# Summing the squares of the RMS norms: from adds on VectorE to accumulating matmuls on TensorE

## The chip, the cores and the metric

The kernel runs on one core of a Trainium2 chip. The metric is device time in microseconds of one execution. "Before" is the kernel as it stands, "after" the one with the change.

## What is computed

A two-layer backbone over 512 latent tokens of width 2048, with 256 context tokens. What matters here is its beginning:

```
shift, scale, gate = split(silu(c) @ w_mod + b_mod, 3)
h  = rmsnorm(x,   g) * (1 + scale)   + shift      # 512 tokens
hc = rmsnorm(ctx, g) * (1 + scale_c) + shift_c    # 256 tokens
rmsnorm(x, g) = x * rsqrt(mean(x*x over the 2048 channels) + 1e-6) * g
```

`h` and `hc` then go through the input projection, windowed attention, a Fourier mixer, the output projection, a pooling layer and a last norm. All of it is float32.

## The kernel before

Channels lie on the 128 partitions and tokens on the free axis, so `x` is 16 tiles (`KT`) of 128 x 512 in `main`, and `ctx` 16 tiles of 128 x 256 in `ctx_t`, which is a part of `kvmem`. The sum over the channels of a token is therefore a sum over 16 tiles and over the partitions; the latter is done by a matmul with `ones` (128 x 128).

The kernel begins with the modulation stage. The first 4096 columns of `l0_w_mod` are streamed as 64 units of 512 KB through four slots of `raw`; a column group `cg` (512 columns, 8 in all) has eight units `s`, each with two channel tiles. For each unit TensorE does two matmuls of 32 condition columns (`cond_cols`, two of them in use) against 512 weight columns. They write 32 of the 128 partitions of bank `cg % 2`, so four tiles of channels land in four partition groups. The unit's last matmul increments `mod_used`, and on that SP (line 276) reloads the slot. When a group is done, ScalarE copies the bank to `mod_rows` (L381), and TensorE turns these rows into columns (`turn_rows`, four small matmuls) behind unit `s == 1` of the next group.

In groups 1 to 4 ScalarE also takes the squares of the 32 tiles, eight in each group (`mod_square`, L322): group 1 and 2 those of `x`, 512 columns wide, group 3 and 4 those of the context, 256 wide. The first square of each kind goes straight into `rstd_x` or `rstd_c` (both in `kvmem`), the others into the two buffers of `tmp`, and VectorE adds them up there (L701). `sq_summed` counts these adds and frees the buffers; `summed_before` gives how many adds stand before a tile. TensorE then sums each of the two over the partitions, with one matmul with `ones` behind unit 3 of group 4 and one behind unit 3 of group 6 (`sum_tokens`), into banks 5 and 6. VectorE waits for both (`tokens_summed`), computes 1 / (mean + eps) (`variance`, L623 and L624), and when all groups are done ScalarE takes the roots (L327). Then come the first two weight splits (L316, L576), the shift and scale vectors, and tile by tile the norm (L627), the split of `h` into two parts (L334, L636) and the first projection.

All engines run their own program in the order written; there is no planner. Every matmul is issued from line 925.

Of the kernel before, what the change touches and what calls it, by code (L numbers as in the profile page):

```python
# [26 lines left out]
SEQ = 512  # L27
CTX = 256
KT = D // P
GROUP = 4  # L30
COLS = GROUP * P
HALVES = KT // 2
# [42 lines left out]
ALU = mybir.AluOpType  # L75
ACT = mybir.ActivationFunctionType
# [48 lines left out]
def build(nc, weights, modb, xT, ctxT, vectors, wf, ident_in, identb_in, masks_in, rope_in, dft_tok_in,  # L125
          dft_ch_in, edges_in, outT):
    with ExitStack() as whole:
        def sb(name, shape, dt, scope=whole):
            return scope.enter_context(nc.sbuf_tensor(name, shape, dt))

        def sem(name):
            return whole.enter_context(nc.semaphore(name))
# [10 lines left out]
        tmp = sb("tmp", [P, 2, WIDE], F32)  # L143
# [3 lines left out]
        ones = ones_r[:].bitcast(F32)  # L147
# [43 lines left out]
        def kv_part(at, shape):  # L191
            n = int(np.prod(shape))
            view = kvmem[:, at:at + n]
            return view if len(shape) == 1 else view.rearrange("p (a b) -> p a b", a=shape[0])
# [13 lines left out]
        rstd_x = kv_part(k_kc, [SEQ])  # L208
        rstd_c = kv_part(k_kc + SEQ, [CTX])
# [5 lines left out]
        ps = whole.enter_context(nc.psum_tensor("ps", [P, 8, 512], F32))  # L215
# [18 lines left out]
        ones_ready, own = sem("ones_ready"), sem("own")  # L234
# [3 lines left out]
        rows_ready, rows_turned = sem("rows_ready"), sem("rows_turned")  # L238
        acc_step, acc_reduced, red_free = sem("acc_step"), sem("acc_reduced"), sem("red_free")
        squared, sq_summed, sq_added = sem("squared"), sem("sq_summed"), sem("sq_added")  # L240
        tokens_summed = sem("tokens_summed")
        ssum_done, var_ready, rstd_ready = sem("ssum_done"), sem("var_ready"), sem("rstd_ready")
        hi_ready, lo_ready, weights_used = sem("hi_ready"), sem("lo_ready"), sem("weights_used")
        tile_ready, split_hi, split_done = sem("tile_ready"), sem("split_hi"), sem("split_done")
# [11 lines left out]
        p_hi_ready, p_ready, p_used = sem("p_hi_ready"), sem("p_ready"), sem("p_used")  # L256
        grp_free = sem("grp_free")
        out_ready = sem("out_ready")

        def summed_before(index):  # L260

            return max(index - 1, 0) if index <= KT else index - 2

        block = whole.enter_context(nc.Block())

# [40 lines left out]
        def _(act):  # L306
# [9 lines left out]
                nc.scalar.copy(w_hi[:, j % 2], raw[:, slot]).then_inc(hi_ready, 1)  # L316

            def square(index, x, n):
                first = {0: rstd_x, KT: rstd_c}.get(index)
                if index >= 2 and summed_before(index - 1):  # L320
                    act.wait_ge(sq_summed, summed_before(index - 1))
                nc.scalar.activation(tmp[:, index % 2, 0:n] if first is None else first, x,  # L322
                                     ACT.Square).then_inc(squared, 1)

            def root(k, dst):
                act.wait_ge(var_ready, k)
# [35 lines left out]
            def mod_square(cg, s):  # L362
                if cg not in range(1, 5):
                    return
                index = HALVES * (cg - 1) + s
                if index == 0:
                    act.wait_ge(x_landed, 64)
                if index == KT:
                    act.wait_ge(ctx_landed, 16)
                if index < KT:  # L370
                    square(index, main[:, index], SEQ)
                else:
                    square(index, ctx_t[:, index - KT], CTX)
# [162 lines left out]
            for g in range(GROUP):  # L536
# [5 lines left out]
                for m in range(GROUP):  # L542
                    t = GROUP * g + m
# [26 lines left out]
        def _(dve):  # L570
# [46 lines left out]
            def variance(k, sums, dst, n):  # L617

                if k > 2:
                    dve.wait_ge(ssum_done, k - 2)  # L620
                if k > 1:
                    dve.wait_ge(var_ready, k - 1)
                chain.link(nc.vector.tensor_scalar(scratch[:, 0:n], sums, 1.0 / D, EPS, ALU.mult, ALU.add))  # L623
                nc.vector.reciprocal(dst, scratch[:, 0:n]).then_inc(var_ready, 1)  # L624
# [67 lines left out]
            chain.link(nc.vector.tensor_tensor(sink_lo[:, :, 0], sinks, sink_hi[:, :, 0].bitcast(F32), ALU.subtract))  # L692


            for index in range(2 * KT):
                if index % KT:
                    dst, n = (rstd_x, SEQ) if index < KT else (rstd_c, CTX)
                    dve.wait_ge(squared, index + 1)
                    if summed_before(index):
                        dve.wait_ge(sq_summed, summed_before(index))  # L700
                    nc.vector.tensor_tensor(dst, dst, tmp[:, index % 2, 0:n], ALU.add).then_inc(sq_summed, 1)  # L701
            dve.wait_ge(tokens_summed, 2)
            variance(1, ps[:, 5], rstd_x, SEQ)
            variance(2, ps[:, 6, 0:CTX], rstd_c, CTX)
            lo(G_K, 0)
# [217 lines left out]
        def _(pe):  # L923
            def mm(out, lhsT, rhs, start, stop):
                return nc.tensor.matmul(out, lhsT, rhs, start=start, stop=stop, skip_group_check=True)  # L925
# [56 lines left out]
                mm(ps[:, 5], ones, ssum, True, True).then_inc(ssum_done, 1)  # L982


            def sum_tokens(index, bank, squares, n):
                pe.wait_ge(sq_summed, summed_before(index))
                mm(ps[:, bank, 0:n], ones, squares, True, True).then_inc(tokens_summed, 1)

            def turn_rows(cg):
                pe.wait_ge(rows_ready, cg + 1)  # L990
                for m in range(GROUP):
                    at = (cg * GROUP + m) * 2
                    ins = mm(ps[:, MOD_BANK, at:at + 2], mod_rows[:, m * P:(m + 1) * P],
                             vec[:, V_ID:V_END], m == 0, True)
                ins.then_inc(rows_turned, 1)

            pe.wait_ge(cond_ready, 1)
            for cg in range(MODS):
                for s in range(HALVES):
                    unit_index = cg * HALVES + s  # L1000
                    pe.wait_ge(raw_landed[unit_index % RAW_SLOTS], (unit_index // RAW_SLOTS + 1) * 16)
                    for r in range(2):
                        kt = 2 * s + r
                        rows = slice(32 * (kt % 4), 32 * (kt % 4) + 32)
                        ins = mm(ps[rows, cg % 2], cond_cols[:, kt], raw[:, unit_index % RAW_SLOTS, r],
                                 kt < 4, kt >= KT - 4)
                    ins.then_inc(mod_used, 1)
                    if s == 1 and cg:
                        turn_rows(cg - 1)
                    if s == 3 and cg == 4:  # L1010
                        sum_tokens(KT, 5, rstd_x, SEQ)
                    if s == 3 and cg == 6:
                        sum_tokens(2 * KT, 6, rstd_c, CTX)
            turn_rows(MODS - 1)


# [142 lines left out]
            for g in range(GROUP):  # L1159
                for kt in range(GROUP):  # L1160
                    s = 2 * g + kt // 2
# [111 lines left out]
```

## Time and profile before

| | |
|---|---|
| Time, median of 3 runs | 1673.22 us (1669.27 to 1677.97) |
| Profiled execution | 1669.27 us, span 1667.6 us |
| Mean granted TensorE clock | 0.960 |
| Busy: TensorE, VectorE, ScalarE, GpSimd | 1507.8, 862.8, 514.8, 67.9 us |
| First unit of the modulation stage starts | 22.75 us |
| Copy of its last group | 125.43 us |

The span is the time between the first and the last instruction of the profiled execution; the time has 1.7 us more around it. Busy times of TensorE count pipelined matmuls, whose ends are modelled. Times of rows are from the span's start.

### The profile page before, as it was taken

What the parts mean: (1) busy time and instruction counts of PE and PEld (TensorE: products, weight loads), DVE (VectorE), ACT (ScalarE), POOL (GpSimd) and SP (SyncE); (2) the same over time, 40 slices, a digit from 0 to 9 for tenths busy, and PEclk for the clock granted to TensorE, in tenths of its full rate; (3) what the DMA queues carried; (4) which work ended last, traced back from release to release, by engine and by line L of the source; (5) the groups of instructions that cost most, each with busy time, mean ns of one, the idle gap of its engine ahead of it and who ended that gap; (6) DMA issues with size and microseconds to landing.
All of it is one profiled execution on the core that took longest, in us unless ns stands there. A gap on an engine that the chain in (4) does not pass through costs nothing.

```text
span 1667.6 us, 19661 instructions
## 1 busy us (share of the span) xinstructions
PE 1507.8 (90%) x6928; PEld 1196.8 (72%) x6928; DVE 862.8 (52%) x1249; ACT 514.8 (31%) x741; POOL 67.9 (4%) x132
## 2 busy tenths in 40 slices
PE   3774999999999999999989997699999999989994
PEld 0114888877775888888878885588877888878883
DVE  1218353455654686777675566633448433353335
ACT  1305141234422343433332222322235222242221
POOL 0000000100010000000001000000000000000000
PEclk9997999999999999999999998799999999999997
DMA  9992434644462233333365555122324332222322
GB/s 343 322 321 89 139 119 162 221 152 162 164 199 82 90 114 100 113 102 112 102 229 187 188 178 174 38 89 100 101 75 151 115 101 88 100 76 101 100 76 101
DMA packets 69062, 232.45 MB, mean 139 GB/s; under 512 B 7328, under 2 KB 10400, under 8 KB 68896
## 3 DMA queue, kind: packets, MB, share of 16 engines
q1 hardware_dynamic: 42624, 151.01, 26.5%
q0 software_dynamic: 18432, 67.12, 12.0%
q10 hardware_dynamic: 7968, 13.82, 2.4%
q8 instruction: 23, 0.38, 0.1%
q14 instruction: 15, 0.12, 0.0%
HBM read 227.73 MB, written 4.19 MB: 139 GB/s over the span
## 4 chain that ended last, share of the span: by engine, by line
PE 74%; DVE 13%; DMA 5%; issue 4%; ACT 3%; ACTq 1%; DVEq 0%; SPq 0%; POOLq 0%
PE ps L925 72%; DMA raw<-in_weights 4%; DVE w_lo L576 2%; ACT tmp L405 1%; PE ps L1112 1%; DVE h_lo L636 1%; DVE scratch L586 1%; DMA modchunk<-in_modb 1%; DVE stat L786 1%; DVE tmp L672 1%; DVE tmp L627 1%; DVE tmp L864 1%; DVE main L627 1%; DVE main L918 1%; DVE pt_lo L804 1%
## 5 line engine op out<-in xcount | busy, mean ns | idle before, releaser
L925 PE MATMUL ps<-h_hi,w_hi 128*128 128x512 f32 x1600 | 639.8, 400 | 64.4 <-DVE w_lo L576 32.4
L925 PE MATMUL ps<-h_lo,w_hi 128*128 128x512 f32 x1600 | 631.2, 394 | 0.0
L925 PE MATMUL ps<-h_hi,w_lo 128*128 128x512 f32 x1600 | 631.1, 394 | 0.0
L576 DVE TENSOR_TENSOR w_lo<-raw,w_hi 128x1024 fp32r<-128x1024 f32 x216 | 264.0, 1223 | 552.3 <-ACT w_hi L316 552.0
L316 ACT CAST w_hi<-raw 128x1024 fp32r<-128x1024 f32 x216 | 226.6, 1052 | 749.9 <-PE ps L925 748.2
L925 PEld LDWEIGHTS ps<-h_hi,w_hi 128*128 128x128 f32 x1600 | 305.8, 191 | 130.8 <-issue 34.9
L925 PEld LDWEIGHTS ps<-h_hi,w_lo 128*128 128x128 f32 x1600 | 305.4, 191 | 65.9
L925 PEld LDWEIGHTS ps<-h_lo,w_hi 128*128 128x128 f32 x1600 | 306.2, 191 | 60.1
L586 DVE SCALAR_TENSOR_TENSOR scratch<-modchunk,cond,scratch 128x512 f32<-128x512 f32 x240 | 179.9, 749 | 22.6 <-DMA modchunk<-in_modb 17.1
L291 POOL DMA_DIRECT2D modchunk<-in_modb x128 | 67.7, 529 | 1225.2 <-DVE scratch L586 1096.4
L925 PE MATMUL ps<-raw,kvmem 128*32 128x512 f32 x256 | 68.1, 702 | 48.8 <-DMA raw<-in_weights 25.8
L925 PEld LDWEIGHTS ps<-raw,kvmem 128*32 128x32 f32 x256 | 9.6, 117 | 98.6 <-DMA raw<-in_weights 74.1
L475 ACT CAST pt_hi<-ps 128x512 fp32r<-128x512 f32 (+1 forms) x48 | 30.7, 640 | 121.6 <-PE ps L1112 121.6
L786 DVE TENSOR_REDUCE stat<-ps 128x1 f32<-128x513 f32 (+1 forms) x48 | 36.3, 756 | 35.4 <-PE ps L925 35.1
L925 PE MATMUL ps<-k_hi,q_hi 128*128 128x256 f32 (+1 forms) x96 | 34.4, 359 | 10.1 <-ACT kvmem L479 5.8
L804 DVE TENSOR_TENSOR pt_lo<-ps,pt_hi 128x512 fp32r<-128x512 f32 (+1 forms) x48 | 36.2, 753 | 8.2 <-ACT pt_hi L475 7.7
L701 DVE TENSOR_TENSOR kvmem<-kvmem,tmp 128x512 f32<-128x512 f32 (+1 forms) x30 | 16.8, 559 | 38.6 <-ACT tmp L322 35.9
L925 PEld LDWEIGHTS ps<-k_hi,q_hi 128*128 128x128 f32 x96 | 18.7, 194 | 17.4 <-ACT kvmem L479 9.3
L405 ACT ACTIVATE tmp<-main 32x512 f32 x48 | 30.2, 630 | 0.7
L925 PE MATMUL ps<-p_hi,w_hi 128*128 128x512 f32 x64 | 26.1, 409 | 3.6 <-issue 3.6
L381 ACT COPY kvmem<-ps 128x512 f32<-128x512 f32 x8 | 4.7, 586 | 79.2 <-PE ps L925 79.2
L444 ACT ACTIVATE tmp<-ps 128x512 f32<-128x512 f32 x32 | 19.2, 599 | 31.6 <-PE ps L925 23.5
(148 smaller groups left out, 1370.5 us busy)
## 6 DMA issues: line engine op xcount, KB each, us to landing
raw<-in_weights SPq DMA_DIRECT2D x280, 512.0 KB, 3.3
modchunk<-in_modb POOLq DMA_DIRECT2D x128, 512.0 KB, 3.6
main<-in_xT ACTq DMA_DIRECT2D x8, 1024.0 KB, 9.1
out<-main SPq DMA_DIRECT2D x16, 256.0 KB, 2.3
kvmem<-in_ctxT ACTq DMA_DIRECT2D x1, 2048.0 KB, 17.5
dft_tok<-in_dft_tok ACTq DMA_DIRECT2D x1, 2048.0 KB, 9.1
kvmem<-in_rope ACTq DMA_DIRECT2D x1, 512.0 KB, 16.1
wf_sb<-in_wf ACTq DMA_DIRECT2D x1, 256.0 KB, 4.1
```

Source lines behind the costliest of these rows:

```text
L291: pool.dma_start(modchunk[:, slot].rearrange("p a n -> p (a n)"), src).then_inc(chunk_landed[slot], 16)
L316: nc.scalar.copy(w_hi[:, j % 2], raw[:, slot]).then_inc(hi_ready, 1)
L405: ins = nc.scalar.activation(tmp[q:q + 32, m % 2, 0:SEQ], view(m)[p:p + 32], ACT.Identity)
L444: nc.scalar.activation(tmp[:, m % 2, 0:SEQ], ps[:, m], ACT.Tanh, scale=0.5).then_inc(tanh_done, 1)
L475: nc.scalar.copy(*turned_tiles(k - 1, pt_hi)).then_inc(pt_hi_ready, 1)
L576: nc.vector.tensor_tensor(w_lo[:, j % 2], raw[:, j % RAW_SLOTS], w_hi[:, j % 2].bitcast(F32), ALU.subtract).then_inc(lo_ready, 1)
L586: ins = nc.vector.scalar_tensor_tensor(out=modacc[:], in0=modchunk[:, s % 2, r], scalar=cond[:, kt, 0:1], in1=modacc[:], op0=ALU.mult, op1 ...
L627: nc.vector.scalar_tensor_tensor(out=dst, in0=x, scalar=g, in1=r, op0=ALU.mult, op1=ALU.mult).then_inc(tile_ready, 1)
L701: nc.vector.tensor_tensor(dst, dst, tmp[:, index % 2, 0:n], ALU.add).then_inc(sq_summed, 1)
L786: chain.link(nc.vector.tensor_reduce(stat[:, 0, par:par + 1], ps_flat[:, S_END - width:S_END], AX.X, ALU.max))
L804: nc.vector.tensor_tensor(lo_part, turned_part, hi_part.bitcast(F32), ALU.subtract).then_inc(pt_ready, 1)
L925: return nc.tensor.matmul(out, lhsT, rhs, start=start, stop=stop, skip_group_check=True)
```

## The change

VectorE no longer adds squares, and each square, now always in `tmp`, is summed over the partitions by a matmul with `ones` of its own. The 16 matmuls of a kind accumulate in bank 5 or 6. On TensorE such a matmul stands right behind each unit of groups 1 to 4 and waits for its square; it increments `sq_summed`, on which ScalarE waits before it overwrites a buffer of `tmp`. VectorE waits for `sq_summed` to reach 32. The two sums at groups 4 and 6, the semaphore `tokens_summed` and `summed_before` are gone, and TensorE waits for `ones_ready` once.

```
 # ScalarE
 def square(index, x, n):
-    first = {0: rstd_x, KT: rstd_c}.get(index)
-    if index >= 2 and summed_before(index - 1):
-        act.wait_ge(sq_summed, summed_before(index - 1))
-    nc.scalar.activation(tmp[:, index % 2, 0:n] if first is None else first, x,
-                         ACT.Square).then_inc(squared, 1)
+    if index >= 2:
+        act.wait_ge(sq_summed, index - 1)
+    nc.scalar.activation(tmp[:, index % 2, 0:n], x, ACT.Square).then_inc(squared, 1)
...
 # VectorE
-for index in range(2 * KT):
-    if index % KT:
-        dst, n = (rstd_x, SEQ) if index < KT else (rstd_c, CTX)
-        dve.wait_ge(squared, index + 1)
-        if summed_before(index):
-            dve.wait_ge(sq_summed, summed_before(index))
-        nc.vector.tensor_tensor(dst, dst, tmp[:, index % 2, 0:n], ALU.add).then_inc(sq_summed, 1)
-dve.wait_ge(tokens_summed, 2)
+dve.wait_ge(sq_summed, 2 * KT)
...
 # TensorE
-def sum_tokens(index, bank, squares, n):
-    pe.wait_ge(sq_summed, summed_before(index))
-    mm(ps[:, bank, 0:n], ones, squares, True, True).then_inc(tokens_summed, 1)
+def mod_square(cg, s):
+    if cg not in range(1, 5):
+        return
+    index = HALVES * (cg - 1) + s
+    t, bank, n = (index, 5, SEQ) if index < KT else (index - KT, 6, CTX)
+    pe.wait_ge(squared, index + 1)
+    mm(ps[:, bank, 0:n], ones, tmp[:, index % 2, 0:n], t == 0, t == KT - 1).then_inc(sq_summed, 1)
+
+pe.wait_ge(ones_ready, 1)
...
         ins.then_inc(mod_used, 1)
+        mod_square(cg, s)
         if s == 1 and cg:
             turn_rows(cg - 1)
-        if s == 3 and cg == 4:
-            sum_tokens(KT, 5, rstd_x, SEQ)
-        if s == 3 and cg == 6:
-            sum_tokens(2 * KT, 6, rstd_c, CTX)
```

## Rows read from the trace of the kernel before

**Rows 1.** The page: busy times; TensorE and DMA in tenths of 40 slices.

```profile
PE 1507.8 (90%) x6928; PEld 1196.8 (72%) x6928; DVE 862.8 (52%) x1249; ACT 514.8 (31%) x741; POOL 67.9 (4%) x132
...
PE   3774999999999999999989997699999999989994
...
DMA  9992434644462233333365555122324332222322
```

**Rows 2.** The chain of waits in order of time: start us, us, what.

```profile
36.81 5.08 PE ps L925 x20
42.92 5.55 DMA raw<-in_weights
...
124.33 1.08 PE ps L925 x4
125.43 0.59 ACT kvmem L381
```

**Rows 3.** Stretches of groups 1 to 5: length, busy times, PEclk, DMA share, GB/s.

```profile
34.20:48.51 14.31, 9.83 (x41) 2.59 (x41) 4.85 (x7) 5.46 (x11) 0.00 (x0) 0.88 0.90 318
48.51:61.80 13.29, 10.60 (x41) 2.27 (x41) 5.54 (x8) 4.95 (x9) 0.00 (x0) 0.74 0.90 309
61.80:74.78 12.98, 9.32 (x40) 2.11 (x41) 3.29 (x8) 4.63 (x12) 0.00 (x0) 1.00 0.95 336
74.78:86.86 12.08, 9.83 (x42) 2.42 (x42) 3.09 (x8) 2.93 (x7) 0.00 (x0) 1.00 0.96 341
86.86:99.42 12.56, 9.33 (x40) 2.12 (x40) 0.00 (x0) 0.48 (x2) 0.00 (x0) 1.00 0.93 320
```

**Rows 4.** Timeline: start us, us, instruction, [idle before <-releaser].

```profile
64.02 0.97 PEld L925 LDWEIGHTS ps<-vec,kvmem 128*128 128x128 f32 x8 [0.84 <-issue]
...
78.84 0.14 PEld L925 LDWEIGHTS ps<-raw,kvmem 128*32 128x32 f32 x4 [0.69 <-DMA raw<-in_weights]
79.82 0.30 PEld L925 LDWEIGHTS ps<-kvmem,ones_r 128*128 128x128 f32 x2 [0.84 <-issue]
...
80.88 0.14 PEld L925 LDWEIGHTS ps<-raw,kvmem 128*32 128x32 f32 x4 [0.76 <-DMA raw<-in_weights]
...
93.53 1.05 PE L925 MATMUL ps<-raw,kvmem 128*32 128x512 f32 x4 [0.67 <-DMA raw<-in_weights]
...
105.27 0.30 PEld L925 LDWEIGHTS ps<-kvmem,ones_r 128*128 128x128 f32 x2 [0.84 <-issue]
...
105.90 0.14 PEld L925 LDWEIGHTS ps<-raw,kvmem 128*32 128x32 f32 x4 [0.33 <-issue]
```

**Rows 5.** One load's issue; landing times, 28 to 125 us; waits in groups 1 to 4.

```profile
82.12 0.33 SPq L270 DMA_DIRECT2D raw<-in_weights  x1
...
DMA to landing us min/median/max: 3.2/5.0/6.3
...
PEld ps L925 <- DMA raw<-in_weights: 39.6, 28, 2.8
```

**Rows 6.** ScalarE at a group's border; the adds on VectorE; VectorE's wait.

```profile
60.53 1.05 PE L925 MATMUL ps<-raw,kvmem 128*32 128x512 f32 x4 [0.26 <-DMA raw<-in_weights]
61.63 0.59 ACT L381 COPY kvmem<-ps 128x512 f32<-128x512 f32 x1 [7.27 <-PE ps L925]
...
62.11 0.42 ACT L322 ACTIVATE kvmem<-kvmem 128x256 f32<-128x256 f32 x1
...
L701 DVE TENSOR_TENSOR kvmem<-kvmem,tmp x30: 424/559/694, 35.5 to 78.2; 128x512 f32<-128x512 f32 x15, 128x256 f32<-128x256 f32 x15
...
106.00 0.69 DVE L623 TENSOR_SCALAR scratch<-ps 128x512 f32<-128x512 f32 x1 [27.38 <-PE ps L925]
```

**Rows 7.** Matmuls with `ones` of the later norms: ns min/median/max, first and last start.

```profile
L925 PE MATMUL ps<-ubuf,ones_r x4: 592/879/1222, 1036.1 to 1648.7; 128*128 128x512 f32 x4
```

**Rows 8.** Timeline of the weight loads around 30 us.

```profile
30.08 0.19 PEld L925 LDWEIGHTS ps<-raw,kvmem 128*32 128x32 f32 x4 [1.09 <-DMA raw<-in_weights]
...
31.36 0.19 PEld L925 LDWEIGHTS ps<-raw,kvmem 128*32 128x32 f32 x4 [1.10 <-DMA raw<-in_weights]
```

More of the change, by code:

```diff
@@ L240, in build @@
         squared, sq_summed, sq_added = sem("squared"), sem("sq_summed"), sem("sq_added")
-        tokens_summed = sem("tokens_summed")
         ssum_done, var_ready, rstd_ready = sem("ssum_done"), sem("var_ready"), sem("rstd_ready")
@@ L258, in build @@
         out_ready = sem("out_ready")
-        def summed_before(index):
-            return max(index - 1, 0) if index <= KT else index - 2
         block = whole.enter_context(nc.Block())
```

## The prediction

> **What bounds the kernel now.** The page comes first [rows 1]. TensorE is busy for 90% of the span, but the slices are uneven: in the first three (some 125 us) TensorE is at 3 to 7 tenths and the DMA engines at 9. The diff works in these slices alone, so the 90% says nothing about it. The second view is the chain of waits in order of time [rows 2]: up to 124.33 us it hops between loads of `raw` of some 4.4 to 5.7 us and short pieces of TensorE, and at 125.43 the copy of the last group on ScalarE takes over. What has to be priced is when the last of the 64 units of the modulation stage is done; all that follows (1667.6 - 125.4 = 1542 us) moves with it, for the work behind it is not edited.
>
> The third view is the table of stretches, one for each column group `cg` = 1 to 5 [rows 3]. Groups 1 to 4, in which the squares are taken, need 14.31, 13.29, 12.98 and 12.08 us, 52.66 in sum; the DMA engines are at 0.90 to 0.96 in them. The timeline shows how a unit looks from close by [rows 4]: four records of 1.05 us in sum, and then idle time that ended with a DMA. What stands beside it is the life of a slot [rows 5]: the unit that starts at 80.88 us lets SP issue the next load at 82.12, so 1.24 us after its start; from issue to landing a load takes 5.0 us in the median, 3.2 at the least. Four slots, so four units take about 1.24 + 5.0 = 6.2 us, eight 12.5: that is the measured group. The stage runs at the pace of this loop, and TensorE has idle time in it. The question is only whether that idle time is as much as the new work.
>
> **The work that moves.** VectorE's 30 adds go: 15 of 0.69 and 15 of 0.43 us, 16.8 us in all [rows 6]. None lies on the chain of waits. VectorE is idle between them for ScalarE, and behind them it waits 27.4 us for the second sum. I price this at nothing; its cover is the rest of the stage, from 106.00, when the variances begin, to the roots behind 125.43 [rows 2, 6]. The variances start earlier now, with no reader who waits. Gone, too, are the two sums on TensorE, of 1.06 us (79.82 to 80.88, the next unit) and 0.63 us (105.27 to 105.90) [rows 4].
>
> Added are 32 matmuls of `ones` against a square, 16 on 512 columns and 16 on 256. These are the same two instructions as the removed sums, so the trace has their price: 1.06 and 0.63 us from start to the next instruction. The two differ by 0.43 us for 256 columns, so 512 columns stream in 0.86 us and some 0.2 us are fixed. The dearest form in the trace is that of the last norms, whose records go from 0.59 to 1.22 us [rows 7]; by it a sum could take up to twice as long, about 2.0 us, and that bound belongs to the lower clock (below). The sum at full clock: 16 × 1.06 + 16 × 0.63 = 27.0 us, less the 1.06 us of the sum that stood in group 4, 26.0 us more on TensorE between 34.20 and 86.86.
>
> A unit itself costs 0.98 us until another instruction can follow (78.84 to 79.82), a row turn 0.97 (64.02) [rows 4]. In the 52.66 us these are 32 × 0.98 + 4 × 0.97 + 1.06 = 36.3 us. TensorE was therefore really idle for 16.3 us, not the 39.6 us that the list of waits gives to its weight loads, since a weight load counts as idle while the matmul runs on [rows 5]. 26.0 us of work do not fit into 16.3 us of gaps: TensorE becomes what sets the pace of groups 1 to 4.
>
> Step by step: unit 8 starts at 34.20 as before and unit 9 at 36.81, since its load was already on the way. From there on no load is awaited: a unit with its 512-column square takes 2.04 us, four of them 8.2 us against 6.2 us for the loop of a slot. In groups 3 and 4 it is 1.61 us, four 6.4 us, still just above, with full slots as a reserve. Units 9 to 39: 31 × 0.98 + 15 × 1.06 + 16 × 0.63 + 4 × 0.97 = 60.2 us, so group 5 starts at 97.0 us where it started at 86.86: 10.2 us late.
>
> Part is given back. When group 5 starts, its four slots have landed and the DMA queue is empty, so the next load needs the least time: unit 44 can start 1.24 + 3.2 = 4.5 us after unit 40, where it took 93.52 - 86.86 = 6.66 us [rows 4, 5]. That is 2.1 us. Behind it the loop is the old one. Net: 10.2 - 2.1 = 8.1 us.
>
> ScalarE's part: `square` now waits for TensorE's sum of two squares earlier instead of VectorE's add. It needs 0.63 or 0.42 us, TensorE asks for one every 2.04 or 1.61 us, so two buffers in `tmp` are ahead of it. At a group's border the copy (0.59 us) and the first square stand in a row: copy at 61.63, first square from 62.11 to 62.53, 2.0 us after unit 23's start at 60.53 [rows 6]; with a 512-column square that is 2.2 us. TensorE asks for it after unit, sum and next unit, 3.0 us (2.6 in the short form). Nothing, with 0.4 to 0.8 us in hand. Behind TensorE's new wait stand the next unit and, through `mod_used`, SP's next load. If that cover were gone it would cost at most 0.6 us at each of four borders. The wait for `ones_ready` costs nothing: filling `ones` is VectorE's first instruction, and TensorE's first unit starts only at 22.75 us. The accumulation over 16 matmuls is interleaved with units in other banks; no price in any row, taken as nothing.
>
> **Clock.** The granted clock was 0.88 and 0.74 in groups 1 and 2, so partly at 1.2 GHz, and 1.00, 2.4 GHz throughout, in groups 3 to 5 [rows 3]. Group 1 has the widest gaps between units (34.20 to 36.81 for one). With TensorE fed all the time I take 2.4 GHz from there on. If the shares stayed as they are, TensorE would lose (1 - 0.88) × 14.31 + (1 - 0.74) × 13.29 = 5.2 us. I price it at nothing and keep the 5.2 us for a rival.
>
> **A rule that prices the square otherwise.** The row gives 1.06 us for 512 columns of fp32, of which 0.86 us scale with the columns. The Trainium skill (FP8 and Floating Point Precision, section TensorE Precision Notes) states four passes through the array for true fp32 and no fixed part; as an estimate from that page the sums would cost the streaming alone. In rows, streaming alone is 0.86 and 0.43 us: units 9 to 39 then take 31 × 0.2 = 6.2 us less, and the kernel loses only 1.9 us. It would need the weights of `ones` to be loaded in the unit's shadow; the 0.84 us in which the weight load stood before 79.82 speak against it [rows 4].
>
> **Against its own time.** Profiled execution: span 1667.6, time 1669.27 us. 1669.3 + 8.1 = 1677.4 us. It is the fastest of the three runs shown; their median is 1673.22, and the same addition to it gives 1681.3 us. I name 1680, nearer to the median. What a measurement of this kernel can tell from no change is about 0.5%, 8.4 us; the forecast, +0.4 to +0.5%, sits just inside that bound.
>
> **Rivals.** *The time is given back (not slower).* The DMA engines are not at their best in the stage: 309 to 341 GB/s, and a unit of group 5 takes 12.56 / 8 = 1.57 us, while those at 30.08 and 31.36 us are 1.28 us apart [rows 3, 8]. If behind the late stage the 24 units of groups 5 to 7 came at 1.28 us, 7.0 us would come back on top, and the time would be 1670 to 1674. It decides from a mean landing time of 3.9 us (four units in 5.1) instead of 5.0. Against it: groups 1 to 5 all had the same four slots, and none came under 12.08 us. Chance 0.2. The Trainium skill (Perfetto Trace Analysis, section Roofline) puts the practical ceiling of a single core at about 435 GB/s; by it there would be room for this rival; the trace shows 341 at most in these groups.
>
> *The square is cheap:* streaming alone, as above, +1.9 us, 1671 to 1675. Chance 0.1.
>
> *The clock stays down or the handshake bites (clearly slower):* the 5.2 us of the clock or the four border stalls of 2.4 us, or both, come on top: 1684 to 1690. If all 60 us ran at the lower level it would be +60 us; for that TensorE would have to be slowed while it is busy, which no row shows. Chance 0.1.
>
> *VectorE's absence speeds up the loads (faster):* without 30 adds the writes into `raw` might be quicker. Groups 3 and 4, with adds, ran at 336 and 341 GB/s, group 5 without at 320 [rows 3]; and while TensorE sets the pace a faster load gains nothing. From the luck of later clock stretches a few us are possible too. 1660 to 1668, chance 0.05.
>
> *The forecast:* 0.55; its own range is 1676 to 1686. Half of its mass is above the bound of 0.5%.
>
> **Numbers.** Faster 0.07 (the last rival and a tail of the first); slower 0.28 of the forecast, 0.1 of the clock, and 0.05 more, 0.43 together, since the median starts 4 us above the trace's own time; the same 0.50. The range of eight in ten runs from the rivals that give the time back, 1671, to the clock's lower end, 1687.
>
> **What the new profile would show.** Groups 1 and 2 of about 17 us, 3 and 4 of 13.9; TensorE without DMA waits from 37 to 97 us; group 5's start at about 97 instead of 86.86; the DMA share down to about 0.75 in groups 1 and 2 (0.90 × 14.31 / 17.3); landings in these of 3.2 to 4 us; granted clock 1.0 there; the copy for the last group at about 133.5 instead of 125.43. Each square's matmuls 1.06 us before the next instruction. I am wrong if units still wait for DMA in groups 1 and 2, if the sum leaves less than 0.9 us between neighbours, or if groups 5 to 7 need less than 36 us together.

## The result and the profile after

Over 16 runs of each, the kernel after takes 1680.49 us in the median (1673.42 to 1684.15), the kernel before 1669.19 us (1664.79 to 1677.97). The ratio is 1.0057, with a 95% interval of 1.0045 to 1.0068: 9.5 us slower (7.5 to 11.4). The two medians themselves are 11.3 us apart, at the upper edge of that interval. The ratio lies just above the 0.5% that the prediction took as its bound, with an interval that reaches below it, and the whole interval is on the slower side of no change.

A warning on the forecast of 1680: it met the median better than it should. It stood on a median of 1673.22 us for the kernel before, which more runs have put at 1669.19; what the working forecast was a loss of 8.1 us, and this is to be held against 9.5 (11.3 by the medians). That the number 1680 came so near is luck: too high a start and too small a loss offset each other.

The page of the kernel after, busy times and tenths of 40 slices, against [rows 1]:

```profile
span 1674.8 us, 19722 instructions
PE 1528.2 (91%) x6988; PEld 1205.0 (72%) x6988; DVE 846.0 (51%) x1219; ACT 515.0 (31%) x741; POOL 67.9 (4%) x132
...
PE   3976799999999999999989998599999999989994
...
DMA  9894333654552332323265555032223322222322
```

VectorE is busy for 16.8 us less, as much as the 30 adds took, and TensorE for 20.4 us more. In the second slice TensorE has gone from 7 to 9, and the first slices of the DMA engines no longer show three 9s.

The stretches of groups 1 to 5 and of group 7, against [rows 3]; columns as there (length, busy time and count of TensorE, weight loads, VectorE, ScalarE, GpSimd, then granted clock, DMA share, GB/s):

```profile
34.13:51.48 17.35, 17.16 (x56) 4.58 (x57) 0.00 (x0) 5.89 (x11) 0.00 (x0) 1.00 0.84 297
51.48:68.57 17.09, 17.09 (x57) 4.58 (x56) 0.00 (x0) 5.42 (x10) 0.00 (x0) 1.00 0.79 240
68.57:82.25 13.68, 13.68 (x57) 4.58 (x56) 0.00 (x0) 3.43 (x9) 0.00 (x0) 1.00 0.83 275
82.25:96.53 14.28, 13.75 (x57) 4.58 (x56) 0.00 (x0) 3.70 (x10) 0.00 (x0) 1.00 0.88 294
96.53:108.97 12.44, 9.06 (x42) 2.12 (x41) 6.22 (x4) 0.22 (x2) 0.00 (x0) 1.00 0.96 325
...
121.90:136.75 14.85, 10.94 (x40) 3.12 (x40) 0.00 (x0) 0.00 (x0) 0.00 (x0) 0.77 0.81 290
```

In group 2 the busy time of TensorE is equal to the length of the stretch, 17.09 of 17.09 us: the engine never waits. The engines that moved 309 GB/s there move 240 now. Group 5 starts at 96.53 us instead of 86.86, so 9.7 us late, and is then as long as before (12.44 against 12.56 us).

The chain of waits in order of time, against [rows 2], tells it in one row. Where it hopped between loads and short pieces of TensorE, it now stays on TensorE for 46.90 us:

```profile
32.16 4.22 DMA raw<-in_weights
...
36.43 46.90 PE ps L911 x166
83.49 6.55 DMA raw<-in_weights
...
92.94 4.97 DMA raw<-in_weights
```

And the timeline of group 2 from close by, against [rows 4]:

```profile
50.42 0.30 PEld L911 LDWEIGHTS ps<-tmp,ones_r 128*128 128x128 f32 x2 [0.84 <-issue]
...
50.54 0.58 ACT L374 COPY kvmem<-ps 128x512 f32<-128x512 f32 x1 [2.40 <-PE ps L911]
...
51.02 1.19 ACT L316 ACTIVATE tmp<-main 128x512 f32<-128x512 f32 x2
51.48 0.14 PEld L911 LDWEIGHTS ps<-raw,kvmem 128*32 128x32 f32 x4 [0.76 <-issue]
...
52.46 0.30 PEld L911 LDWEIGHTS ps<-tmp,ones_r 128*128 128x128 f32 x2 [0.84 <-ACT tmp L316]
...
53.52 0.14 PEld L911 LDWEIGHTS ps<-raw,kvmem 128*32 128x32 f32 x4 [0.76 <-issue]
```

Sum at 50.42, unit at 51.48, sum at 52.46, unit at 53.52: 1.06, 0.98, 1.06 us. One must not be misled by the label "<-ACT tmp L316" at 52.46. The two squares begun at 51.02 were over at 52.21, 0.25 us before; the 0.84 us ahead of the weight load are the unit's own matmuls, and they are as long where the label is "issue". ScalarE is the engine that waits:

```profile
ACT tmp L316 <- PE ps L911: 34.6, 24, 2.2
...
PEld ps L911 <- ACT tmp L316: 18.4, 22, 0.8
PEld ps L911 <- DMA raw<-in_weights: 1.9, 2, 1.0
```

Between 36.4 and 96.5 us TensorE's weight loads wait for a DMA for 1.9 us in two places; in groups 1 to 4 of the kernel before it was 39.6 us in 28 [rows 5].

### The profile page after: what moved, and what is told of

It is laid out like the page before. It is cut to its first block, busy times and chain, and to the rows that moved or that the text cites. A ratio compares the mean times of both kernels' runs of the same rounds, so it can differ in the third digit from the quotient of the medians.

```text
span 1674.8 us, 19722 instructions
## 1 busy us (share of the span) xinstructions
PE 1528.2 (91%) x6988; PEld 1205.0 (72%) x6988; DVE 846.0 (51%) x1219; ACT 515.0 (31%) x741; POOL 67.9 (4%) x132
## 4 chain that ended last, share of the span: by engine, by line
PE 75%; DVE 13%; issue 4%; DMA 3%; ACT 3%; ACTq 1%; DVEq 0%; SPq 0%; POOLq 0%
PE ps L911 74%; DMA raw<-in_weights 3%; DVE w_lo L569 2%; ACT tmp L398 1%; PE ps L1100 1%; DVE h_lo L629 1%; DVE scratch L579 1%; DVE stat L772 1%; DVE tmp L665 1%; DVE tmp L620 1%; DVE tmp L850 1%; DVE main L620 1%; DVE main L904 1%; DVE pt_lo L790 1%; DMA modchunk<-in_modb 1%
## 5 line engine op out<-in xcount | busy, mean ns | idle before, releaser
L911 PE MATMUL ps<-tmp,ones_r 128*128 128x512 f32 (+1 forms) x64 | 29.2, 538 | 0.0
```

## The experiments

The question was what the loss consists of: TensorE's own time for the sums, beyond its gaps (theory 1), the wait of TensorE for ScalarE's squares (theory 2), or, in the later ones, a limit of the engines. Ratios are to the kernel before on the same chip, with 95% intervals.

**Sums of two columns.** All sums but the first of each kind stream 2 columns. Most columns of the sums are left out, so the norms differ from the reference's.

```
+                n = n if t == 0 else 2
                 mm(ps[:, bank, 0:n], ones, tmp[:, index % 2, 0:n], t == 0, t == KT - 1).then_inc(sq_summed, 1)
```

> The change with every sum but the first of each kind streaming 2 columns instead of 512 or 256; it leaves out most columns of the sums, so the norms are not the reference's. All waits and semaphores stay. Theory 1 (TensorE's streaming time beyond its gaps is the loss): a unit with its sum costs about 0.98 + 0.2 us, below the 1.57 us of the slot loop, so group 5 starts at 86 to 88 us and the ratio to before is 0.998 to 1.002. Theory 2 (the wait of TensorE for ScalarE's squares is the loss): group 5 still starts at 96 to 97 us and the ratio stays at 1.0057.

Measured: 1670.84 us, ratio 1.001 (0.9995 to 1.0025). The timeline of its weight loads, and its groups 1 and 2:

```profile
53.27 0.30 PEld L911 LDWEIGHTS ps<-tmp,ones_r 128*128 128x128 f32 x2 [0.84 <-issue]
53.59 0.14 PEld L911 LDWEIGHTS ps<-raw,kvmem 128*32 128x32 f32 x4
...
34.80:48.80 14.00, 12.28 (x56) 4.42 (x56) 0.00 (x0) 5.72 (x11) 0.00 (x0) 1.00 0.92 329
48.80:61.66 12.86, 11.47 (x57) 4.43 (x57) 0.00 (x0) 5.41 (x10) 0.00 (x0) 1.00 0.93 334
```

With all 32 waits in place and without the streaming, the loss is gone; group 5 starts at 88.73 us, 0.7 us past my mark, but in groups 3 and 4 of that run the granted clock was 0.92 and 0.96. Theory 2 falls. A sum of 2 columns still takes 0.32 us (53.27 to 53.59), of which its two weight loads fill 0.30. That is a floor for a narrow sum, and more than the 0.2 us that I had put down as the fixed part. The run also has none of VectorE's adds, so these cost or gave nothing beyond the interval.

**Every sum twice.** The sums are twice too large.

```
-                mm(ps[:, bank, 0:n], ones, tmp[:, index % 2, 0:n], t == 0, t == KT - 1).then_inc(sq_summed, 1)
+                mm(ps[:, bank, 0:n], ones, tmp[:, index % 2, 0:n], t == 0, False)
+                mm(ps[:, bank, 0:n], ones, tmp[:, index % 2, 0:n], False, t == KT - 1).then_inc(sq_summed, 1)
```

> The change with every sum done twice into the same accumulation, so the sums are twice too large. Theory 1: 27 us more on TensorE with no gap left to take them: group 5 starts at 120 to 124 us, ratio to before 1.020 to 1.023. Theory 2: the handshake is hidden behind the second matmul, so less is added than is issued: group 5 starts under 112 us, ratio under 1.015.

Measured: 1698.49 us, ratio 1.0169 (1.0149 to 1.0189). Both numbers of theory 1 were too high, and both of theory 2 too low, so the ranges alone don't decide; the trace does. The timeline of its weight loads and its groups 2 and 4:

```profile
50.72 0.30 PEld L911 LDWEIGHTS ps<-tmp,ones_r 128*128 128x128 f32 x2 [0.84 <-ACT tmp L316]
51.25 0.19 PEld L911 LDWEIGHTS ps<-tmp,ones_r 128*128 128x128 f32 x1 [0.24 <-issue]
51.68 0.19 PEld L911 LDWEIGHTS ps<-tmp,ones_r 128*128 128x128 f32 x1 [0.24 <-issue]
52.63 0.14 PEld L911 LDWEIGHTS ps<-raw,kvmem 128*32 128x32 f32 x4 [0.76 <-issue]
...
58.42:82.38 23.96, 23.96 (x73) 7.62 (x72) 0.00 (x0) 5.31 (x9) 0.00 (x0) 1.00 0.51 174
...
99.52:116.65 17.13, 17.13 (x73) 7.62 (x73) 0.00 (x0) 3.50 (x8) 0.00 (x0) 1.00 0.73 245
```

Two wide sums take 52.63 - 50.72 = 1.91 us, the second only 0.85: its weights are loaded while the first streams, and the fixed part, 1.06 - 0.85 = 0.21 us, is paid once. TensorE is busy for all 23.96 us of group 2, so nothing there waits for a square. 16 × 0.85 + 16 × 0.43 = 20.5 us should then be added, and group 5 starts at 116.65 instead of 96.53, 20.1 us later. What I had wrong was the price of the second sum. TensorE's time is passed on to the start of group 5 one for one; the ratios agree roughly (1.0169 - 1.0057 is 18.7 us, each with an interval of some 2 to 3 us to either side).

**Sums spread.** Wide sums behind every second unit of groups 1 to 4, short ones behind each unit of groups 5 and 6; the second edit below is made in ScalarE's program and in TensorE's.

```
+def tile_at(unit):
+    if HALVES <= unit < 5 * HALVES and unit % 2 == 0:
+        return (unit - HALVES) // 2
+    if 5 * HALVES <= unit < 7 * HALVES:
+        return unit - 5 * HALVES + KT
+    return None
...
-                if cg not in range(1, 5):
-                    return
-                index = HALVES * (cg - 1) + s
+                index = tile_at(HALVES * cg + s)
+                if index is None:
+                    return
```

> The change with the sums spread: those of x behind every second unit of groups 1 to 4, those of the context behind every unit of groups 5 and 6. Theory 1: two units and one wide sum take 2 x 0.98 + 1.06 + 0.24 = 3.3 us against 3.1 us of the slot loop, a unit with a short sum 1.73 against 1.57; the last copy comes 2 to 4 us later than before, ratio 1.001 to 1.003. Theory 2: each of the 32 waits still costs the same, ratio 1.004 or more. A third view, that any work in the stage is lost because TensorE is in the loop of the slots (a unit's end gives the next load): the full 26 us less a few, ratio above 1.010.

Measured: 1673.94 us, ratio 1.002 (1.0009 to 1.0031). Group 1, group 6 and the last copy:

```profile
34.01:47.75 13.74, 13.25 (x50) 3.35 (x48) 0.00 (x0) 3.03 (x6) 0.00 (x0) 1.00 0.91 332
...
101.88:115.64 13.76, 13.76 (x58) 4.58 (x57) 0.00 (x0) 3.78 (x10) 0.00 (x0) 1.00 0.87 295
...
127.83 0.59 ACT L383 COPY kvmem<-ps 128x512 f32<-128x512 f32 x1 [12.20 <-PE ps L920]
```

The same 27 us of sums cost 2.4 us at the last copy (127.83 against 125.43 [rows 2]) when they find gaps of their own size. Even so TensorE is busy throughout group 6, 13.76 us. The third view falls too: work in a gap is not lost.

**One pass.** ScalarE rounds the squares to fp32r, and the sum is an fp32r matmul. In the trace an fp32 sum is two pairs of weight load and matmul (x2 in the lines above), an fp32r sum is one; these pairs are meant by "pass" here.

```
-                nc.scalar.activation(tmp[:, index % 2, 0:n], x, ACT.Square).then_inc(squared, 1)
+                nc.scalar.activation(h_hi[:, KT - 2 + index % 2, 0:n], x, ACT.Square).then_inc(squared, 1)
...
-                mm(ps[:, bank, 0:n], ones, tmp[:, index % 2, 0:n], ...
+                mm(ps[:, bank, 0:n], ones_r[:], h_hi[:, KT - 2 + index % 2, 0:n], ...
```

> The change with the squares rounded to fp32r by ScalarE (into two tiles of h_hi, free in this stage) and summed as fp32r, one pass instead of two. Theory 1: a wide sum costs 0.3 to 0.5 us instead of 1.06, a unit with it 1.3 to 1.5 us, so the stage is again set by the slot loop: group 5 at 86 to 88 us, ratio 0.998 to 1.002. Theory 2: same waits, ratio 1.0057.

Measured: 1672.66 us, ratio 1.0013 (0.9997 to 1.0029). Its weight loads and its group 2:

```profile
52.93 0.19 PEld L911 LDWEIGHTS ps<-h_hi,ones_r 128*128 128x128 f32 x1 [0.84 <-issue]
53.36 0.14 PEld L911 LDWEIGHTS ps<-raw,kvmem 128*32 128x32 f32 x4 [0.24 <-issue]
...
48.34:61.35 13.01, 12.15 (x50) 3.62 (x49) 0.00 (x0) 5.43 (x10) 0.00 (x0) 1.00 0.88 310
```

A wide sum takes 0.43 us instead of 1.06, TensorE has gaps again, and what is left of the loss is not clear of zero. The order of the work and the waits are those of the kernel after.

**Eight slots, with the kernel before.** The modulation stage gets four more slots in memory that is free then.

```
+MOD_SLOTS = 8
-MOD_ROUNDS = MOD_UNITS // RAW_SLOTS
+MOD_ROUNDS = MOD_UNITS // MOD_SLOTS
...
+        def mod_slot(i):
+            if i < RAW_SLOTS:
+                return raw[:, i]
+            return pooled[:, 2 * (i - RAW_SLOTS):2 * (i - RAW_SLOTS) + 2]
...
+            for j in range(MOD_SLOTS):
+                load(weights[j], j)
+            with sp.Fori(1, MOD_ROUNDS) as q:
+                for j in range(MOD_SLOTS):
+                    sp.wait_ge(mod_used, q * MOD_SLOTS + (j + 1 - MOD_SLOTS))
+                    load(weights[q * MOD_SLOTS + j], j)
```

> The kernel before with eight slots for the modulation stage instead of four (four more in the memory of pooled, free then). If the stage is set by the loop of a slot (1.24 us and a landing of 5.0 us for four units), a deeper queue lets the loads run at the rate of the engines, 1.28 to 1.4 us a unit instead of 1.57: last unit at 108 to 114 us instead of 124.33, ratio 0.990 to 0.994. If the engines are at their limit already (share 0.90 to 0.96), nothing changes: ratio 0.999 to 1.001.

Measured: 1651.05 us, ratio 0.9888 (0.9871 to 0.9904). Groups 2 and 5, landing times of 30 to 105 us, and the last copy:

```profile
44.42:55.70 11.28, 8.87 (x40) 2.12 (x40) 5.54 (x8) 5.40 (x10) 0.00 (x0) 1.00 1.02 407
...
76.19:86.57 10.38, 8.87 (x40) 2.12 (x40) 0.00 (x0) 0.73 (x2) 0.00 (x0) 1.00 1.03 407
...
DMA to landing us min/median/max: 3.9/9.0/10.0
...
106.88 0.59 ACT L391 COPY kvmem<-ps 128x512 f32<-128x512 f32 x1 [9.65 <-PE ps L935]
```

The loop of a slot did set the pace before: with eight, six of seven groups take 10.0 to 10.5 us, 1.3 us a unit. Now it is the engines that do, at 407 GB/s and over, and a load waits in their queue (9.0 us; 1.24 + 9.0 = 10.2 us for eight units). The stage ends 18.6 us earlier, although its first unit, at 27.85 us, comes 5 us later than before, so my 108 to 114 us for the last unit (it starts at 105.8) was too careful, and so was my ratio.

**Eight slots, with the kernel after, and with one pass.**

> The kernel after with eight slots. TensorE sets the pace of groups 1 to 4 as before, so group 5 starts at 95 to 97 us; then eight landed units wait instead of four, and groups 5 to 7 run at 1.3 us a unit: last unit at 119 to 124 us, ratio to before 0.997 to 1.000, and 10 to 13 us behind the eight-slot form of the kernel before: the sums cost more once the loads are faster. If instead the engines are at their limit with four slots already, eight slots change nothing behind group 5 either, ratio 1.0057.

> Eight slots and the one-pass sums on fp32r squares. A unit with its wide sum takes 0.98 + 0.43 = 1.41 us, close to the 1.3 us of the loads: last unit at 110 to 114 us, ratio 0.991 to 0.994, within 3 us of the eight-slot form of the kernel before. If eight slots don't speed up the loads: ratio 1.000 to 1.002, as with four slots.

Measured: 1669.56 us, ratio 0.9996 (0.9986 to 1.0007), and 1653.47 us, ratio 0.9897 (0.9881 to 0.9914). Of the first, groups 2, 5 and 6 and the last copy:

```profile
51.02:68.11 17.09, 17.09 (x57) 4.58 (x56) 0.00 (x0) 5.42 (x10) 0.00 (x0) 1.00 0.75 247
...
95.47:102.95 7.48, 5.67 (x42) 1.92 (x41) 6.22 (x4) 0.66 (x2) 0.00 (x0) 1.00 0.92 315
102.95:113.15 10.20, 8.87 (x40) 2.12 (x40) 0.00 (x0) 0.19 (x1) 0.00 (x0) 1.00 1.03 416
...
124.72 0.59 ACT L384 COPY kvmem<-ps 128x512 f32<-128x512 f32 x1 [11.17 <-PE ps L921]
```

Of the second, group 3 and the last copy:

```profile
59.30:70.47 11.17, 11.17 (x49) 3.54 (x48) 0.00 (x0) 3.60 (x10) 0.00 (x0) 1.00 0.95 372
...
109.02 0.59 ACT L384 COPY kvmem<-ps 128x512 f32<-128x512 f32 x1 [9.65 <-PE ps L921]
```

With faster loads the fp32 sums cost 124.72 - 106.88 = 17.8 us at the last copy, where they cost some 11 with four slots: groups 1 to 4 stand where they stood (17.09 us for group 2, to the hundredth), while the pace they are held against has risen. I had expected 10 to 13 us; groups 1 to 4 of the form without them became shorter than I had reckoned. The one-pass form is 2.1 us behind; its last unit starts at 107.92 us, before the 110 I had named, and its ratio is below my range. So the form with VectorE's adds and eight slots has the lowest time of all, though its interval overlaps that of the one-pass form.

**The kernel after once more.**

> The kernel after once more, for a second profile. In its first profile group 5 started 9.7 us late and the last unit 11.4 us late, the 1.7 us more arising in group 7 around a stretch at the lower clock. If groups 1 to 4 are set by TensorE alone, group 5 starts at 96.5 us again, within 0.3 us; if the 1.7 us of group 7 are a matter of chance, the last unit stands elsewhere, between 133 and 136 us. Ratio 1.0045 to 1.0068, as before.

Measured: 1679.96 us, ratio 1.0062 (1.0044 to 1.0081). Groups 2, 3 and 4 of the second profile, and its last copy:

```profile
51.82:68.91 17.09, 17.09 (x57) 4.58 (x57) 0.00 (x0) 5.42 (x10) 0.00 (x0) 1.00 0.78 248
68.91:82.59 13.68, 13.68 (x57) 4.58 (x57) 0.00 (x0) 3.43 (x9) 0.00 (x0) 1.00 0.86 266
82.59:96.27 13.68, 13.68 (x58) 4.59 (x57) 0.00 (x0) 3.71 (x10) 0.00 (x0) 1.00 0.89 305
...
135.92 0.58 ACT L375 COPY kvmem<-ps 128x512 f32<-128x512 f32 x1 [14.14 <-PE ps L912]
```

Group 5 starts at 96.27 us, 0.26 from the first profile, and the last unit at 133.95 instead of 135.69. Group 4 takes 13.68 us, as group 3 does; the 14.28 of the first profile hold a stop of 0.6 us for a load at 90.04. What TensorE sets, repeats in these two profiles; what the loads set, scatters: from the start of group 5 to the last copy it was 38.6 us before, 40.3 and 39.7 in the two profiles of the kernel after, but 37.4 with narrow sums, 37.0 with one pass and 37.6 with doubled ones.

## Why the prediction was right, point by point

**The bound of the stage.** That the loop of four slots sets the pace and not the engines was read from 1.24 + 5.0 us; eight slots have shown it.

**The price of a sum.** 1.06 and 0.63 us were right to the hundredth, and they sufficed for group 5: forecast 97.0, measured 96.53 and 96.27. A row turn behind a sum costs less than the 0.97 us taken for it: sum and turn together need 1.41 us (84.85 to 86.26) instead of 0.63 + 0.97, and four such turns make up most of the difference. The split of 1.06 into 0.86 and 0.2 held as well: the second of two sums took 0.85. Only a narrow sum doesn't shrink to the 0.2, since its weight loads alone take 0.30. The rival of the cheap square falls: its condition, weights loaded in the shadow, holds behind another sum and not behind a unit. The Trainium skill (FP8 and Floating Point Precision, section TensorE Precision Notes) names four passes and no fixed part. An estimate from it, four times 512 columns at 2.4 GHz with one column in a cycle, is 0.85 us; the second of two sums took just that, but the section leaves out what the change from a unit to a sum costs.

**Gaps against work.** 26.0 us into 16.3: right in kind and size. Groups 1 to 4 took 17.35, 17.09, 13.68 and 14.28 us, forecast about 17 and 13.9. The 39.6 us of waits of weight loads would have told the opposite. The sum over instructions showed the true gap, and TensorE's busy times in [rows 3] leave nearly the same, 13.1 us of the 52.7 without a matmul.

**What is given back.** Here a term failed. I forecast 2.1 us, on the ground that the DMA queue is empty when group 5 starts and the next load lands after 3.2 us. Unit 44 started at 102.69 us, 6.16 us after unit 40, so 0.5 us came back (6.04 us and 0.6 in the second profile). From 96.5 to 103 us loads took as long to land as ever:

```profile
DMA to landing us min/median/max: 4.9/5.2/5.8
```

The slots had not all landed and the queue was not empty: the load that unit 41 waits for was issued at 92.94 us and landed at 97.91, 1.4 us after unit 40 had started. In the second profile unit 41 waited for its load too, until 98.19. The likely reason, which no run tests by itself, is that in groups 3 and 4 TensorE needs 6.4 us for four units and the loop 6.2, so that little reserve was left at their end; in the first profile a load of 6.55 us even stopped TensorE until 90.04 us. With 0.5 in place of 2.1 the sum is 9.7 us, against a measured 9.5 (7.5 to 11.4).

**The rest of the profile.** The last copy stands 11.4 us later than before in the first profile (136.79 against 125.43) and 10.5 us later in the second (135.92), more than group 5's delay of 9.7 and 9.4. In the first the rest behind it is 4.2 us shorter (1674.8 - 136.8 = 1538.0 against 1542.2 us), so the span is only 7.2 us longer; in the second the rest takes 1541.3 us, and the span is 9.6 us longer. Whether the stage's last third is a little slower in the kernel after, or both are scatter, stays open; the experiments with 37.0 to 37.6 us there speak for scatter.

**Rivals.** The time was not given back with four slots, nor with eight: there group 5 took 7.48 us, thanks to eight landed units, but of 19.3 us at its start 17.8 were left at the end. The clock did not stay down, it was 1.00 in groups 1 to 5. The handshake cost nothing that can be measured: a narrow sum with the same waits ran at 1.001 (0.9995 to 1.0025). And nothing shows the loads to run faster for VectorE's absence: 329 and 334 GB/s in groups 1 and 2 with narrow sums against 318 and 309, but 317 and 284 in groups 3 and 4 against 336 and 341.

**Details that were off.** The DMA share was 0.84 and 0.79 where I had 0.75, landings between 36.4 and 68 us took 3.3 to 4.8 us where I had 3.2 to 4, and the copy of the last group came at about 136 instead of 133.5 us, by the term above and by the scatter. Groups 5 to 7 took 40.2 us, so that sign of being wrong stayed away. The chances leaned a little to "the same" (0.50 against 0.43); the ratio came out just beyond the bound.

## What to carry to other kernels

Moving work onto an engine that has gaps in a transfer-bound stage is free only while the gap of each buffer's turn takes the work of that turn: add up the engine's own instructions from start to start, and don't take the idle time that the list of waits shows for the weight loads. Spreading the same work over more turns, or making it cheaper per turn, won back nearly everything here (2.4 us left of some 11). And where a stage loads at the pace of its slots, the number of slots can be worth more than the engine on which a sum is done: 1.1% here against 0.6%.

## What the runs showed of the hardware that I had not expected

The DMA share is no measure of what the engines can still do. At 0.90 to 0.96 with up to four loads of 512 KB in flight they moved 309 to 341 GB/s [rows 3]; with up to eight, in the kernel before, they moved 407 to 411 GB/s at a share of 1.02 to 1.03. The Trainium skill (Perfetto Trace Analysis, section Identifying the Most-Contended Engine) says to judge DMA by the use of the memory's bandwidth instead of occupancy, and these runs agree. As an estimate by its ceiling of some 435 GB/s for a core that runs alone (section Roofline), four slots left about a fourth unused and eight leave 6%.

A matmul with `ones` over 128 columns of the array costs about 0.2 us more behind a unit that used 32 columns (1.06 us for 512 moving columns) than behind its like (0.85 us). With 2 moving columns it still takes 0.32 us. Rounding the moving operand to fp32r and running the sum as fp32r brought 512 columns from 1.06 to 0.43 us, start to start.
